# The gates of layer 1's mixing stage as seven products of half-size blocks, in fp32 on one Trainium2 core

## The reference, cut to what matters

```
def merge_branches(branches, gate_logits, w_branch, w_out):
    gates = jax.nn.sigmoid(gate_logits)
    merged = gates[..., :D_MODEL] * (branches[0] @ w_branch[0])
    for i in range(1, N_BRANCH):
        merged = merged + gates[..., i * D_MODEL:(i + 1) * D_MODEL] * (branches[i] @ w_branch[i])
    return merged @ w_out
```

## Time and profile before

| | us |
|---|---|
| median of 3 runs | 2875.28 |
| lowest and highest | 2872.45, 2875.68 |
| the profiled execution | 2874.93 |
| its span | 2873.1 |
| TensorE busy | 2720.6 |
| VectorE busy | 1352.1 |

### The profile page before, as it was taken

The page is one execution under the profiler, slowest core; times in us unless marked ns, Lnnn a source line. Parts: engine busy times, 40 slices in busy tenths (PEclk is TensorE's granted clock), DMA queues, the critical chain, the costliest instruction groups (busy, mean ns, idle before and its releaser), DMA issues.

```text
span 2873.1 us, 42275 instructions
## 1 busy us (share of the span) xinstructions
PE 2720.6 (95%) x17528; PEld 1977.1 (69%) x17528; DVE 1352.1 (47%) x2753; ACT 436.4 (15%) x873; POOL 75.4 (3%) x137
## 2 busy tenths in 40 slices
PE   7999999999898899999988998899999999999998
PEld 3544444576666667788644444488788998988997
DVE  3956656532222234684311111179634764843763
ACT  0222210210000012231100000011321201022110
POOL 0100012000000000000100000000000000000000
PEclk9999999999999999999999999999999999999999
DMA  9623348389999975233899999944232443333441
GB/s 376 201 103 121 132 141 344 121 338 421 421 410 421 421 313 167 95 119 147 349 421 421 421 385 421 421 176 156 99 133 103 172 166 132 135 139 116 159 164 45
DMA packets 114765, 685.48 MB, mean 239 GB/s; under 512 B 20752, under 2 KB 22032, under 8 KB 39712
## 3 DMA queue, kind: packets, MB, share of 16 engines
q1 hardware_dynamic: 84144, 600.79, 52.8%
q0 software_dynamic: 16992, 69.54, 6.6%
q10 hardware_dynamic: 13456, 12.59, 1.6%
HBM read 679.46 MB, written 3.41 MB: 238 GB/s over the span
## 4 chain that ended last, share of the span: by engine, by line
PE 37%; DMA 14%; DVE 1%; issue 0%; ACT 0%; SPq 0%; DVEq 0%; ACTq 0%
PE ps L774 14%; DMA ring<-units 13%; PE ps L746 12%; PE ps L1215 2%; PE ps L1517 2%; PE ps L1339 2%; PE ps L1479 1%; DMA early_values<-arena 1%; PE ps L1371 0%; PE ps L1351 0%; PE ps L1081 0%; PE ps L809 0%; PE ps L783 0%; PE ps L792 0%; PE ps L1269 0%
## 5 line engine op out<-in xcount | busy, mean ns | idle before, releaser
L1215 PE MATMUL ps<-ring,arena 128*32 128x256 f32 x2928 | 359.5, 382 | 46.2 <-DMA ring<-units 44.9
L1200 PE MATMUL ps<-ring,arena 128*64 128x256 f32 x2960 | 339.3, 381 | 44.5 <-DMA ring<-units 44.2
L1200 PEld LDWEIGHTS ps<-ring,arena 128*64 128x64 f32 x2960 | 226.6, 137 | 148.2 <-issue 64.6
L1215 PEld LDWEIGHTS ps<-ring,arena 128*32 128x32 f32 x2928 | 175.6, 109 | 222.0 <-DMA ring<-units 91.2
L746 PE MATMUL ps<-h,ring 128*128 128x256 f32 (+1 forms) x992 | 250.5, 415 | 10.9 <-ACT h L1696 9.9
L746 PEld LDWEIGHTS ps<-h,ring 128*128 128x128 f32 x992 | 192.1, 194 | 68.2 <-issue 42.5
L1040 PE MATMUL ps<-u,ring 128*128 128x512 f32 (+1 forms) x544 | 235.0, 586 | 1.9 <-DVE arena L2335 1.9
L1040 PEld LDWEIGHTS ps<-u,ring 128*128 128x128 f32 x544 | 103.2, 192 | 127.3 <-issue 126.0
L2671 DVE COPY u<-ps 32x512 f32<-32x512 f32 (+1 forms) x128 | 70.8, 553 | 208.4 <-PE ps L1215 115.6
L746 PE MATMUL ps<-arena,ring 128*128 128x256 f32 x640 | 139.5, 379 | 1.3 <-DVE arena L3105 1.3
L746 PEld LDWEIGHTS ps<-arena,ring 128*128 128x128 f32 x640 | 121.4, 190 | 18.1 <-DVE arena L2998 1.7
(11 more groups left out here) (499 smaller groups left out, 3945.2 us busy)
## 6 DMA issues: line engine op xcount, KB each, us to landing
ring<-units SPq DMA_DIRECT2D x568, 1024.0 KB, 13.4
slots<-turned_mod POOLq DMA_DIRECT2D x62, 512.0 KB, 5.3
arena<-turned_mod POOLq DMA_DIRECT2D x18, 512.0 KB, 11.7
arena<-quarters ACTq DMA_DIRECT2D x32, 256.0 KB, 2.9
arena<-units POOLq DMA_DIRECT2D x7, 1024.0 KB, 7.0
h<-tokens SPq DMA_DIRECT2D x4, 512.0 KB, 12.2
arena<-neighbours ACTq DMA_DIRECT2D x32, 64.0 KB, 8.8
arena<-tokens ACTq DMA_DIRECT2D x1, 2048.0 KB, 13.0
```

Of the source, the lines that this page charges most:

```text
L1200: last = nc.tensor.matmul(ps[j * slots:(j + 1) * slots, bank, lo:lo + UC], lhsT[:, kt, 0:slots], row_of(w[j], kt), start=(kt == 0), stop=( ...
L1215: last = nc.tensor.matmul(ps[j % 4 * slots:(j % 4 + 1) * slots, banks[j // 4], 0:UC], lhsT[:, kt, 0:slots], row_of(w[j], kt), start=(kt == ...
```

## The change

Chunk 0 of layer 1 stays as it was. In chunks 1 to 15 the gate unit is cut into two-by-two blocks: 512 of the 1024 input rows, 128 of the 256 output columns, 256 of the 512 columns of `u`. Seven products of such blocks (4 matmuls of 256 columns each) take the place of eight. The sums:

- Four sums of token blocks, once, in chunk 0 after the first softmax, in ring slots 4 and 5.
- Four sums of weight blocks for the next chunk (`sum_wide_weights`), in each chunk from 0 to 14, in ring slots 6 and 7 in turn. The ring keeps slots 0 to 3 for units 16 to 35, and units 36 to 39 are loaded after the last merge.
- The sums of product blocks, in SBUF in `gate`: ScalarE copies the first product, VectorE adds the second and sixth (`early_blocks`), the fifth inside the second softmax (`add_fifth`), the third and seventh and, after the last of TensorE's seven, two more (`late_blocks`).
- One Tanh of 1024 elements out of SBUF, after them, in place of two out of PSUM.

The branch products now wait for `gates_added`, the last product for `wide_fifth_added`, the fifth for the merge of the chunk before. `MOD_MIX` is (1, eleven times 2, 9, 9, 9, 4) in place of (1, ten times 3, 3, 10, 10, 9, 0); the nine tiles that are left follow the last merge. POOL issues them as far ahead as before.

```diff
-MOD_MIX = (1,) + 10 * (3,) + (3, 10, 10, 9, 0)
+MOD_MIX = (1,) + 11 * (2,) + (9, 9, 9, 4)
+GATES, NARROW = 15, 35
+def slot_of(n):
+    return n % (RING // 2) if GATES < n < NARROW else n % RING
...
+            for n in range(2 * RING, NARROW + 5):
+                if n < 2 * RING + RING // 2:
+                    sp.wait_ge(units_used, n - RING + 1)
+                elif n <= NARROW:
+                    sp.wait_ge(units_used, n - RING // 2 + 1)
+                else:
+                    sp.wait_ge(merged_step, 16)
+                sp.dma_start(ring[:, slot_of(n), :], units[n]).then_inc(loaded[n % RING], 16)
...
+                def gate_products(c):
+                    w = unit()
+                    s, t = wide_weight_sums[c % 2], wide_token_sums
+                    def product(bank, half, lhsT, rhs):
+                        for k in range(4):
+                            last = nc.tensor.matmul(ps[:, bank, half * S:(half + 1) * S], lhsT[:, k, :], rhs[:, k, :],
+                                                    start=(k == 0), stop=(k == 3))
+                        return last
+                    pe.wait_ge(gate_kept, 2 * c)
+                    product(gb + 1, 0, w[:, 0:4, 0:P], u[:, 0:4, 0:S]).then_inc(wide_first_ready, 1)
+                    product(gb, 0, w[:, 4:8, 0:P], u[:, 4:8, 0:S])
+                    pe.wait_ge(wide_tokens_summed, 1)
+                    pe.wait_ge(wide_weights_summed, c)
+                    product(gb, 1, s[1], t[1]).then_inc(wide_early_ready, 1)
+                    attend(2 * c)
+                    pe.wait_ge(merged_step, c)
+                    product(wb + 1, 1, s[0], t[0]).then_inc(wide_fifth_ready, 1)
+                    product(wb, 1, s[2], t[2])
+                    product(wb, 0, s[3], u[:, 4:8, S:]).then_inc(wide_late_ready, 1)
+                    pe.wait_ge(wide_fifth_added, c)
+                    product(wb + 1, 0, w[:, 4:8, P:UC], t[3]).then_inc(units_used, 1)
...
+                    if l == 0 and chunk:
+                        exps(2 * chunk)
+                        act.wait_ge(wide_first_ready, chunk)
+                        A(first_product_kept, ps[:, gb + 1, 0:S], ACT.Copy).then_inc(wide_first_kept, 1)
+                        next_quarter(chunk)
+                        copies(2 * chunk)
+                        exps(2 * chunk + 1)
+                        copies(2 * chunk + 1)
+                        act.wait_ge(gates_added, chunk)
+                        A(gate[:, :, 0:T], gate[:, :, 0:T], ACT.Tanh, scale=0.5).then_inc(gate_kept, 2)
...
+                        if chunk < 15:
+                            sum_wide_weights(chunk + 1)
+                        if chunk:
+                            early_blocks(chunk)
+                            softmax(2 * chunk + 1, add_fifth)
+                            late_blocks()
+                        else:
+                            softmax(2 * chunk + 1)
                         modulation_tiles(MOD_MIX[chunk] - MOD_MIX[chunk] // 2, chunk)
...
                 merge(15)
+                if l == 0:
+                    modulation_tiles(MOD_TILES - sum(MOD_PREPARE) - sum(MOD_MIX), 16)
```

More of the change, by code:

```diff
@@ L363, in build @@
         rtmp = part(10752, 4, S)
+        wide_token_sums = [part(1024 * (i % 2), 4, S, of=ring[:, 4 + i // 2, :]) for i in range(4)]
+        wide_weight_sums = [[part(4 * P * i, 4, P, of=ring[:, 7 - q, :]) for i in range(4)] for q in range(2)]
+        gate_blocks = gate.rearrange("p j n -> p (j n)")
+        first_product_kept = small[:, 512:512 + S]
         merged = [h, h[:, :, S:]]
@@ L630, in _ @@
             pool.wait_ge(conditions_ready, 1)
-            modulation_tiles(0, MOD_LATE + MOD_SLOTS)
-            pool.wait_ge(mixed, 24)
-            modulation_tiles(MOD_LATE + MOD_SLOTS, MOD_TILES)
+            used = sum(MOD_PREPARE)
+            issued = used + MOD_SLOTS
+            modulation_tiles(0, issued)
+            for chunk in range(15):
+                used += MOD_MIX[chunk]
+                upto = min(used + (MOD_SLOTS if used < MOD_LATE else len(tile_slots)), MOD_TILES)
+                if issued <= MOD_LATE + MOD_SLOTS < upto:
+                    pool.wait_ge(mixed, 24)
+                modulation_tiles(issued, upto)
+                issued = upto
+            modulation_tiles(issued, MOD_TILES)
             for l in range(DEPTH):
@@ L1020, in mix_branches @@
                     done = 16 * l + chunk
-                    sevens = l == 1 and chunk > 0
-                    if sevens:
+                    if l and chunk:
                         if chunk == 1:
@@ L2478, in merge, with sum_wide_weights, early_blocks, add_fifth @@
                         v.tensor_tensor(m, m, t, ALU.add).then_inc(merged_step, 1)
+                first, second, third, fourth = [gate_blocks[:, n * S:(n + 1) * S] for n in range(4)]
+                def sum_wide_weights(c):
+                    n, to = GATES + c, wide_weight_sums[c % 2]
+                    w = ring[:, slot_of(n), :].rearrange("p (k c) -> p k c", c=UC)
+                    dve.wait_ge(loaded[n % RING], 16 * (n // RING + 1))
+                    dve.wait_ge(units_used, max(n - 1, GATES))
+                    v.tensor_tensor(to[0], w[:, 0:4, P:UC], w[:, 4:8, P:UC], ALU.add).then_inc(dve_step, 1)
+                    v.tensor_tensor(to[2], w[:, 0:4, 0:P], w[:, 0:4, P:UC], ALU.subtract)
+                    dve.wait_ge(dve_step, at(dve_step))
+                    link(v.tensor_tensor(to[1], to[0], w[:, 0:4, 0:P], ALU.subtract))
+                    v.tensor_tensor(to[3], w[:, 4:8, 0:P], to[1], ALU.subtract).then_inc(wide_weights_summed, 1)
+                def early_blocks(chunk):
+                    dve.wait_ge(merged_step, chunk)
+                    dve.wait_ge(wide_first_kept, at(wide_first_kept))
+                    dve.wait_ge(wide_early_ready, at(wide_early_ready))
+                    link(v.tensor_tensor(gate[:, :, 0:S], ps[:, gb, :].rearrange("p (a n) -> p a n", n=S),
+                                         wide(first_product_kept, [P, 2, S]), ALU.add))
+                def add_fifth():
+                    dve.wait_ge(wide_fifth_ready, at(wide_fifth_ready))
+                    v.tensor_tensor(second, third, ps[:, wb + 1, S:], ALU.add).then_inc(wide_fifth_added, 1)
+                def late_blocks():
+                    dve.wait_ge(wide_fifth_added, at(wide_fifth_added))
+                    dve.wait_ge(wide_late_ready, at(wide_late_ready))
+                    link(v.tensor_tensor(gate_blocks[:, S:3 * S], gate_blocks[:, S:3 * S], ps[:, wb, :], ALU.add))
+                    dve.wait_ge(units_used, at(units_used))
+                    count.skip(units_used, -1)
+                    link(v.tensor_tensor(fourth, third, ps[:, wb + 1, S:], ALU.add))
+                    v.tensor_tensor(third, third, ps[:, wb + 1, 0:S], ALU.add).then_inc(gates_added, 1)
                 for chunk in range(16):
```

44 lines of the change are left out of this document (29 added, 15 removed).

## The result

The changed kernel takes 2879.66 us (median of 20 runs, 2875.08 to 2883.57); the kernel before, run beside it, 2874.27 us (20 runs). The ratio is 1.0017, with an interval of 1.0011 to 1.0023: slower by 5.4 us, 0.17 to 0.19%. 2882.5 was forecast; the bound of the prediction for "slower" was 0.2%, so the time lies just on the other side of it, in "no change" (given 0.32, slower 0.58). The profiled execution spans 2878.0 us, against 2873.1.

The account below looks back on a forecast made before the run. TensorE, 95% busy, was taken to bound the kernel, with VectorE setting the pace in the tail after the change. +1.7 - 15.0 - 2.5 + 18.5 + 4.5 = +7.2 us gave 2882.5 us, range 2874 to 2891.

Parts of the forecast that it names:

- slower: Whole kernel: time more than 0.2% (5.75 us) above the kernel before; chance 0.58.
- TensorE's saving and the light chunks: Chunks 1, 2, 3, 6, 7, 10, 11: 1.62 us of products and a 0.53 us wait saved each, 15.0 us.
- Chunks 4, 5, 8, 9: Full-width masked chunks: VectorE's round sets the pace, 92.4 us in place of 94.9, so -2.5 us.
- Chunk 0: Token and weight sums ahead of the second softmax end it at 160.0 instead of 158.3, +1.7 us.
- The tail: Chunks 12 to 15: VectorE's two-pass tiles and sums delay last products, 87.9 us against 69.5, +18.5 us.
- VectorE near 100% busy from chunk 12 to 14: Sign expected in the trace of chunks 12 to 14 if VectorE sets the tail.
- Landing: Tail tiles through three slots: at 4.1 us only chunk 13's single tiles wait (1.4); at 7.3, +7.5 us.
- rival (e): Chunks 12 to 15: tiles stay hidden as now, clock never falls; 2856 us, half way 2868; chance 0.10.
- Rival (c): Chunks 12 and 13: tiles land late, costing three times the excess over 4.8 us; 2890 us at 7.3; chance 0.12.
- The clock: Chunks 12 to 14: TensorE's idles drop its granted clock, slowing work behind them; +4.5 us from 0 to 6.5.
- At nothing: Behind the stage: nine tiles after the last merge, 10.8 us, covered by the output product; four-slot ring also costs nothing.
- The sum: All terms together: +7.2 us on the profiled 2874.93, 2882.1; 2882.5 for the median.

Follow-up runs that it names:

- f4: Changed kernel with seven half-size products in chunks 1 to 11 alone, chunks 12 to 15 computing gates as the kernel before, table unchanged: 2866.68 us, ratio 0.9972.
- h1: f4 with the nine tile slots open from tile 42 on instead of tile 51: 2855.30 us, ratio 0.9928.
- h3: The kernel before with the changed kernel's table of tiles and the nine slots open from tile 42: 2873.72 us, ratio 0.9993.
- f2: Changed kernel with the old table of tiles (3 a chunk in most early chunks, then 3, 10, 10, 9, 0): 2891.02 us, ratio 1.0060.
- f1: Changed kernel with four modulation tiles in each of chunks 12 to 15, 24 behind the last merge instead of nine: 2881.75 us, ratio 1.0027.
- i2: Changed kernel with five half-size products more, rewriting the same numbers, three in chunk 12 and two in chunk 13: 2879.11 us, ratio 1.0021.
- i3: Changed kernel with VectorE's copy of the last mixed values moved behind chunk 12's first four tiles: 2876.78 us, ratio 1.0014.
- h4: Changed kernel with all tiles of chunks 12 to 15 behind the three sums of the gates, where four stood ahead: 2896.78 us, ratio 1.0070.
- f3: The kernel before with the changed kernel's table of tiles alone, gates as sixteen matmuls of 512 columns: 2881.68 us, ratio 1.0030.
- i1: Changed kernel with the nine tile slots open from tile 42 on instead of tile 51: 2876.00 us, ratio 1.0005.
- i4: Changed kernel with 6, 6, 6 and 5 tiles in chunks 12 to 15, 17 behind the last merge, slots open from tile 42: 2870.39 us, ratio 0.9989.

## Why the prediction was right, and where it wasn't

**TensorE's saving and the light chunks: right.** 14.9 us for 15.0. A product was 1.73 us (sixteen records 3.46 from start to start), and the ScalarE waits of the earlier trace rows fell from 4.3 to 1.0 us. f4 shows that it doesn't hang on the tail, and h1 against h3 that it reaches the end undiminished.

**Chunks 4, 5, 8, 9: right.** 3.0 us for 2.5. f2 adds what a third tile does there (10.3 us over the four, where its passes are 9.6), so VectorE's chain did set their pace: the chain, with its waits for ScalarE's exponentials, and not the load, for VectorE is busy 76 of the 91.9 us. The sum 92.4 is partly luck. It leaves out the fifth block, which the prediction had priced at 0.36, 1.4 us over the four; with it the forecast would have been 93.9, so the rest of the round was put 2 us too high.

**Chunk 0: right.** +1.6 for +1.7.

**The tail: right in size, and mostly in its places.** 23.3 us for 18.5 + 4.5; chunk by chunk 27.9, 26.6, 21.4, 16.9 against 25.8, 25.9, 19.6, 16.6 before the clock. The idles stand where they were forecast, except chunk 13's second (1.89 for 4.7): the fifth and sixth products ahead of it were slowed by 2.9 us, which came out of the idle. f1, i2 and i3 carry the mechanism: fewer tiles shorten the tail by 16.7 us, 8.7 us more of TensorE work lengthen it by 0.4, and 3.3 us of idle taken from VectorE bring the last products 3.1 us forward.

**A wrong sign beside it.** "VectorE near 100% busy from chunk 12 to 14" failed: 62.7 of 75.9 us. I had added up one chain and read it as one engine's load. Part of that chain runs over TensorE's products (15.6 us of VectorE's waits from 401 to 494 us are for TensorE), and h4, where I trusted the load and expected no change, came out 15 to 17 us slower.

**Landing: right here, and no guide to a faster tail.** "At 4.1 only chunk 13's single tiles wait" (1.4) is what happened: VectorE waits 1.7 us, at chunk 13's single tiles. But rival (e) let the tail's tiles "stay hidden as now", and f3 says that they would not, even with no sums: the table alone makes the tail 6.7 us longer. Landing was priced only for the changed kernel, where the slow pace of the sums gives it time; for a faster tail three slots are too few. Rival (c) had the right place and the wrong kernel: the changed one waited 1.7 us for tiles, f3 14.0, f4 16.8.

**The clock: right.** 4.5 us for what rows of the tail show: 1.7 us at chunk 12's last product, 2.9 in chunk 13, 1.5 in chunk 14, 6.1 us of slowed work, some of which hides. What doesn't can be read from the chunks: they came out 2.1, 0.7, 1.8 and 0.3 us above the forecast without the clock, 4.9 in all. The 4.5 was a choice in a range of 0 to 6.5, and i1 to i3 show that slowed stretches move, so that it fits to half a microsecond is partly luck. Outside the stage I had counted nothing, and there the profiled execution gained 3.3 and lost 1.7 us.

**At nothing: right.** The nine tiles behind the merge end at 507.3 us, the scaling at 509.95 (16 us after the stage, as forecast), and TensorE's first 80 records of the output product run without a wait. f1 and i4 bound that cover: with 17 tiles TensorE doesn't wait either, with 24 it waits 17.67 us.

**The sum.** +7.2 us on the span for a stage that lost 7.1. The median moved by 5.4 us and the profiled span by 4.9; in the profiled run the difference is the clock at layer 2's start; for the median no row tells it. The time came out 2.8 us below the forecast and inside the range. The chance was on the wrong side by little: "slower" had 0.58, and 5.4 us are just under its bound of 5.75; the interval, 0.11 to 0.23%, holds the bound.

## What to carry to other kernels

Work that moves from the full engine to the half-empty one has to fit in each stretch, not on average: here eleven chunks took it for 18 us of gain and four gave back 23, and using it only in the eleven, with buffers opened early enough for the others, made 2875.8 us into 2855.3.
When a table of background work is changed together with the kernel, run the table alone: in the kernel before it cost 6.7 us by itself, and in f4, which has no sums in the tail, 11 us, all by tiles that arrive through three slots. Opening the slots earlier, without other change, took both away.
Filling an idle with dummy work, and moving one waiting instruction, tell more surely who sets the pace than a share of busy time does.

## What the runs showed of the hardware

The same idle does not always cost the same. All 14 profiled kernels idle 1.90 us before layer 2's first gate product. In the kernel before, h3 and i1 the next sixteen records took 5.38 us (granted clock in the kernel before 0.68 from 1159.9 to 1165.2 us, so a part at the lower of the two levels, 1.2 GHz); in the other eleven 3.69 us (1.00 in the changed kernel). I found nothing in the rows just ahead of them that differs but the time at which they come. I have no run that tells what decides it, so it stays open. It is worth 1.7 us in those records, and in the kernel before 3.3 us with the slowed rows behind them, which h3 and i1 don't have: as much as the effects that were measured in i1 and i3; changes of 2 or 3 us in one profile of this kernel mean little without the median.

A slowed stretch also moves rather than goes: i2 and i3 cut the idle before one product, and another stretch (the branch products, 5.91 and 5.62 us for 3.67) ran slowly instead.

Transfers that run beside each other share what is moved: in f1, with SyncE's units issued up to 503.2 us, 512 KB tiles came every 3.76 us (139 of the 356 GB/s from 500 to 520 us, at a DMA share of 0.87), where VectorE takes one in 1.2 us.
